# A decoder trunk in split fp32: the order of TensorE's products within groups of four weight blocks

## The reference

```python
def swiglu(h, w_in, w_out):
    gate, up = jnp.split(h @ w_in, 2, axis=-1)
    return (jax.nn.silu(gate) * up) @ w_out

for i in range(DEPTH):                     # DEPTH = 2, N_A = 1
    x = x + 0.5 * swiglu(rms_norm(x, ffn1_norm[i]), ffn1_w_in[i], ffn1_w_out[i])
    hm = rms_norm(x, mix_norm[i])
    if i < N_A:
        x = x + retention(hm, ret_w_in[i], ret_w_out[i])
    else:
        x = x + window_attention(hm, k_sh, v_sh, attn_w_q[j], q_norm[j], attn_sinks[j], attn_w_o[j])
    x = x + 0.5 * swiglu(rms_norm(x, ffn2_norm[i]), ffn2_w_in[i], ffn2_w_out[i])
    if i == N_A - 1:
        k_sh, v_sh = shared_kv(x, kv_norm, kv_w, k_norm)
```

## Time and profile before

| | us |
|---|---|
| median of 3 runs | 1044.52 (1043.75 to 1046.14) |
| profiled execution | 1044.49 |
| its span, first to last instruction | 1042.7 |
| PE busy | 1018.2 |
| PE weight loads busy | 884.8 |
| DVE busy | 797.1 |
| ACT busy | 499.4 |
| POOL busy | 110.0 |

### The profile page before, as it was taken

The page is one execution under the profiler, slowest core; times in us unless marked ns, Lnnn a source line. Parts: engine busy times, 40 slices in busy tenths (PEclk is TensorE's granted clock), DMA queues, the critical chain, the costliest instruction groups (busy, mean ns, idle before and its releaser), DMA issues.

```text
span 1042.7 us, 15888 instructions
## 1 busy us (share of the span) xinstructions
PE 1018.2 (98%) x5826; PEld 884.8 (85%) x5826; DVE 797.1 (76%) x953; ACT 499.4 (48%) x537; POOL 110.0 (11%) x102
## 2 busy tenths in 40 slices
PE   7999999999999999999999999999997699999998
PEld 6888888888888888888888888888886588888887
DVE  6977876788788688877766887788679768787743
ACT  5544544544444264544444455454447836454432
POOL 6000013201100151000023000001320040000000
PEclk9999999999999999999999999999998899999999
DMA  9655356652543454555456464544662134554461
GB/s 337 233 183 200 134 170 210 260 215 89 217 181 122 161 182 173 210 181 185 149 182 230 165 234 165 198 140 160 210 252 88 41 115 168 207 196 157 148 195 63
DMA packets 31281, 185.21 MB, mean 178 GB/s; under 512 B 3728, under 2 KB 5264, under 8 KB 14992
## 3 DMA queue, kind: packets, MB, share of 16 engines
q1 hardware_dynamic: 31248, 184.80, 49.9%
HBM read 183.73 MB, written 1.05 MB: 177 GB/s over the span
## 4 chain that ended last, share of the span: by engine, by line
PE 93%; DVE 3%; ACT 2%; DMA 1%; issue 0%; POOL 0%; SPq 0%; POOLq 0%; DVEq 0%; ACTq 0%
PE ps L1031 92%; PE ps L1294 1%; DMA stage<-w_in_dram 1%; ACT w_hi L301 1%; DVE h L625 1%; DVE w_lo L589 0%; ACT s_two L509 0%; DVE s_two L869 0%; ACT s_two L519 0%; ACT s_own L509 0%; DVE q_a L719 0%; DVE w_lo L949 0%; DVE q_b L716 0%; DVE s_own L869 0%; DVE q_a L713 0%
## 5 line engine op out<-in xcount | busy, mean ns | idle before, releaser
L1031 PE MATMUL ps<-h,w_hi 128*128 128x512 f32 x1664 | 585.3, 397 | 4.9 <-DVE h L625 3.0
L1031 PE MATMUL ps<-h,w_lo 128*128 128x256 f32 x1664 | 464.0, 279 | 0.0
L589 DVE TENSOR_TENSOR w_lo<-stage,w_hi 128x2048 fp32r<-128x2048 f32 (+1 forms) x191 | 399.1, 2098 | 29.5 <-ACT w_hi L301 29.2
L1031 PEld LDWEIGHTS ps<-h,w_hi 128*128 128x128 f32 x1664 | 313.3, 188 | 79.1 <-issue 3.3
L301 ACT ACTIVATE w_hi<-stage 128x2048 fp32r<-128x2048 f32 (+1 forms) x191 | 328.4, 1727 | 10.0 <-PE ps L1031 9.1
L1031 PEld LDWEIGHTS ps<-h,w_lo 128*128 128x128 f32 x1664 | 314.0, 189 | 0.3
L1031 PE MATMUL ps<-act_t,w_hi 128*128 128x512 f32 x704 | 245.4, 395 | 0.0
L1031 PE MATMUL ps<-act_t,w_lo 128*128 128x256 f32 x704 | 195.7, 278 | 0.0
L1031 PEld LDWEIGHTS ps<-act_t,w_hi 128*128 128x128 f32 x704 | 132.1, 188 | 31.3
L325 ACT ACTIVATE tmp<-ps 128x1024 f32<-128x1024 f32 x44 | 45.2, 1026 | 193.8 <-PE ps L1031 193.8
L1031 PEld LDWEIGHTS ps<-act_t,w_lo 128*128 128x128 f32 x704 | 132.3, 188 | 0.0
(11 more groups left out here) (150 smaller groups left out, 754.6 us busy)
## 6 DMA issues: line engine op xcount, KB each, us to landing
stage<-w_in_dram SPq DMA_DIRECT2D x86, 1024.0 KB, 4.8
stage<-w_out_dram SPq DMA_DIRECT2D x64, 704.0 KB, 4.1
stage<-w_ret_dram SPq DMA_DIRECT2D x24, 1024.0 KB, 4.8
stage<-w_ret_out_dram SPq DMA_DIRECT2D x8, 1024.0 KB, 4.8
stage<-w_q_dram SPq DMA_DIRECT2D x4, 1024.0 KB, 4.8
stage<-w_o_dram SPq DMA_DIRECT2D x4, 1024.0 KB, 4.9
stage<-w_in_dram SPq DMA_DIRECT2D x4, 256.0 KB, 6.1
x<-x_t_dram SPq DMA_DIRECT2D x4, 256.0 KB, 6.2
```

Of the source, the lines that this page charges most:

```text
L589: nc.vector.tensor_tensor(w_lo[:, s, 0:n], stage[:, s, 0:n], w_hi[:, s, 0:n].bitcast(F32), ALU.subtract).then_inc(lo_ready, 1)
L1031: return nc.tensor.matmul(out_, w, x_, start=start, stop=stop)
```

## The change

The helper `weight_block` is split into `hi_product` (the 512-column matmul) and `lo_product` (the 256-column one). All its callers take the blocks in groups of four: first the four 512-column matmuls, then the four 256-column ones. The w_out units with 11 blocks have groups of 4, 4 and 3. In `pair` a group is two tiles of h times two banks. Products, operands, banks and slots are the same, and each bank still gets its 512-column product first.

```diff
-            def weight_block(bank, slot, b, moving, first, last):
-
-                cols = slice(b * P, (b + 1) * P)
-                matmul(ps[:, bank, :], w_hi[:, slot, cols], moving, first, False)
-                return matmul(ps[:, bank, 0:T], w_lo[:, slot, cols], moving[:, 0:T], False, last)
+            def hi_product(bank, slot, b, moving, first):
+                return matmul(ps[:, bank, :], w_hi[:, slot, b * P:(b + 1) * P], moving, first, False)
+
+            def lo_product(bank, slot, b, moving, last):
+                return matmul(ps[:, bank, 0:T], w_lo[:, slot, b * P:(b + 1) * P], moving[:, 0:T], False, last)
...
                         for o in range(4):
-                            last = weight_block(4 * (g % 2) + o, (u + part) % SLOTS, 4 * k + o, h[:, kt, :],
-                                                kt == 0, kt == DT - 1)
+                            hi_product(4 * (g % 2) + o, (u + part) % SLOTS, 4 * k + o, h[:, kt, :], kt == 0)
+                        for o in range(4):
+                            last = lo_product(4 * (g % 2) + o, (u + part) % SLOTS, 4 * k + o, h[:, kt, :],
+                                              kt == DT - 1)
...
-                            for b in range(FT // 2):
-                                k = FT // 2 * part + b
-                                if d == 0 and k % 2 == 0:
-
-                                    if k in (0, 10, 18, 20):
+                            for b0 in range(0, FT // 2, 4):
+                                blocks = range(b0, min(b0 + 4, FT // 2))
+                                for b in blocks:
+                                    k = FT // 2 * part + b
+                                    if d == 0 and k in (0, 10, 18, 20):
+
                                         pe.wait_ge(a_ready, CREDIT + GROUPS * f + {0: 5, 10: 9, 18: 10, 20: 11}[k])
-                                last = weight_block(4 + d, u % SLOTS, b, act_t[:, k, :], k == 0, k == FT - 1)
+                                    hi_product(4 + d, u % SLOTS, b, act_t[:, k, :], k == 0)
+                                for b in blocks:
+                                    k = FT // 2 * part + b
+                                    last = lo_product(4 + d, u % SLOTS, b, act_t[:, k, :], k == FT - 1)
                             last.then_inc(used, 1)
...
-                for k in range(DT):
-                    if u == FIRST["ret", 0]:
-
-                        pe.wait_ge(h_lo, DT * RET + k + 1)
-                    for o in range(2):
-                        last = weight_block(banks + o, u % SLOTS, 2 * k + o, h[:, k, :], k == 0, k == DT - 1)
+                for k0 in range(0, DT, 2):
+                    blocks = [(k, o) for k in (k0, k0 + 1) for o in range(2)]
+                    for k, o in blocks:
+                        if u == FIRST["ret", 0] and o == 0:
+
+                            pe.wait_ge(h_lo, DT * RET + k + 1)
+                        hi_product(banks + o, u % SLOTS, 2 * k + o, h[:, k, :], k == 0)
+                    for k, o in blocks:
+                        last = lo_product(banks + o, u % SLOTS, 2 * k + o, h[:, k, :], k == DT - 1)
                 last.then_inc(used, 1)
```

More of the change, by code:

```diff
@@ L1206, in retention @@
                     pe.wait_ge(lo_ready, u0 + d + 1)
-                    for k in range(half):
-                        weight_block(d, (u0 + d) % SLOTS, k, y_t[:, k, :], k == 0, False)
+                    for k0 in range(0, half, 4):
+                        for k in range(k0, k0 + 4):
+                            hi_product(d, (u0 + d) % SLOTS, k, y_t[:, k, :], k == 0)
+                        for k in range(k0, k0 + 4):
+                            lo_product(d, (u0 + d) % SLOTS, k, y_t[:, k, :], False)
                     if d == 0:
@@ L1215, in retention @@
                         pe.wait_ge(lo_ready, u0 + d + 1)
-                    for k in range(half if d < 4 else 0, YT):
-                        last = weight_block(d, (u0 + d) % SLOTS, k, y_t[:, k, :], k == 0, k == YT - 1)
+                    for k0 in range(half if d < 4 else 0, YT, 4):
+                        for k in range(k0, k0 + 4):
+                            hi_product(d, (u0 + d) % SLOTS, k, y_t[:, k, :], k == 0)
+                        for k in range(k0, k0 + 4):
+                            last = lo_product(d, (u0 + d) % SLOTS, k, y_t[:, k, :], k == YT - 1)
                     last.then_inc(used, 1)
@@ L1324, in wo_unit @@
                         continue
-                    for k, kt in enumerate(kts):
-                        last = weight_block(d, u % SLOTS, len(kts) * n + k, o_t[:, kt, :], kt == 0, kt == DT - 1)
+                    for k0 in range(0, len(kts), 4):
+                        for k in range(k0, k0 + 4):
+                            hi_product(d, u % SLOTS, len(kts) * n + k, o_t[:, kts[k], :], kts[k] == 0)
+                        for k in range(k0, k0 + 4):
+                            last = lo_product(d, u % SLOTS, len(kts) * n + k, o_t[:, kts[k], :], kts[k] == DT - 1)
                     if j and d != tiles[-1]:
```

## The result

The changed kernel took 1050.14 us (median of six runs, 1047.11 to 1050.64), the kernel before 1044.24 in the same comparison. The ratio is 1.0047 with a 95% interval of 1.0034 to 1.0061: slower, by more than the 0.2% that a measurement of this kernel can tell. A second comparison in five rounds gave 1048.53 us and 1.0046 [1.0022, 1.0070]. The profiled execution took 1050.08 us, its span 1048.3.

A forecast was written before the change was run, and what follows sets the result against it. TensorE's distance between matmul starts was taken to bound the kernel. Terms 1 and 3 counted zero and term 2 saved 4.2 us, so 1044.49 became 1040.3 us, with a range of 1035.5 to 1050.

The forecast's parts named there:

- Term 1: Fast stretches: a group of four stays at 1387 ns, seams -7 to +13 ns a group, taken as zero; nothing gained.
- Term 2: Slow stretches in third FFN and retention heads: 632 blocks fall to the even step, 6.7 ns each, 4.2 us saved.
- Term 3: Waits for act_t (w_out units) and h (first retention unit) move up 0.12 and 0.24 us; slack covers them, no cost.
- the slow cadence spreads: New PSUM banks or seams slow 1928 weight blocks from 346.7 to 353 ns: 1057.3 us, mild form 1048.8; chance 0.22.
- The break-even: Weight blocks: the kernel averages 348.3 ns a block, so 1.6 ns over the even step decides between faster and slower.
- Seams give something back: Every 256-to-512 seam takes 0.113 us, unrepaid: 640 groups save another 6.7 ns each, 4.3 us, 1036.0 us; chance 0.12.
- Both cadences stay: Groups of four don't clear the entry's state; slow stretches stay slow, fast ones fast: 1044.5 us; chance 0.24.
- the mild case: Half the slow spread everywhere, 13.3 ns a group, 4.3 us more: 1048.8 us; half of the 0.22 chance.

## Why the prediction was wrong, point by point

**Term 1, the fast stretches, is the step that failed.** It held that equal-width steps would cost 226.7 and 120.0 inside a group and bounded the two seams from single steps, -7 to +13 ns a group, taking zero. Measured: +16.7 ns a group in w_in units, outside the bound, and some +9 in w_out units, inside its upper end but not zero. The bound looked at the one step on the seam. The disturbance behind a seam is five wide steps long, and a step ahead of it is no witness for the steps behind it. The rows had it: in the earlier trace rows the alternating stretch behind token_block begins with 0.23 and 0.11 and only then slows down. The sum "226.7 + 120.0 = 346.7, the fast cadence to the decimal" was a coincidence of totals: in the fast alternation no step is even (231, 112, 233, 117), and its long and short steps just cancel. Groups of four break that balance. Three FFNs lost 1.8 to 1.9 us each by it, 5.5 in all.

**Term 2, the slow stretches, was right in direction and too large.** The groups did end the slow cadence wherever it was, and in the FFNs one pace holds whatever the entry. But that pace is 350.8 and 349.1, not 346.7; the even step that it expected in each group is not reached by the wide products of a group of four. In the third FFN's w_in units the gain was 2.5 ns a block instead of 6.7, 0.8 us of 2.2, and in its w_out units 0.7 of 1.2. Retention, where 0.9 were expected, lost 0.3 with its output.

The profiled 1050.08 us is 9.8 over the forecast of 1040.3. By the traces 5.5 of that come from term 1; 1.8 in the third FFN and 1.1 in retention from what term 2 had promised; 1.2 from the start and 0.2 from attention, which the sum had not moved.

**Term 3 was right.** TensorE waits for no act_t anywhere in the changed kernel, and for h only in the start. It had left out that the wait of block 18 moves further than that of block 20, by three narrow products or 0.36 us; that operand was in time as well.

**The rivals.** The mild form of "the slow cadence spreads", 1048.8 us at a chance of half of 0.22, came nearest. Of its two mechanisms the second, a seam that throws the pipeline off, is close to what happens, although the pipeline goes into a disturbance of its own and not into the slow pattern; the first, a dearer step at each new bank, is refuted by the w_out units and by the two kernels without a change of width. The break-even it named, 1.6 ns over the even step, was passed with 4.2 in w_in and 2.5 in w_out units. "Seams give something back" was half true: the wide-to-narrow seam does return 8 ns, and the other takes 28. "Both cadences stay" was false in the trace, although its time would have been a closer guess than the forecast.

**The range** ended at 1050.0, a tenth of a microsecond under the median. It took in the mild case only at its single price of 1048.8. That price was half of an assumed worst case, so that it came near is luck, with the start of the program left as traced; the starts of the traces here differ by 2.7 us.

## What to carry to other kernels

When products of different widths take turns on TensorE, the price is in the sequence and not in the instruction. Read the distance between starts over several whole periods, and don't build a new sequence from single steps of an old one: the disturbance behind a change of width reaches five products on. Of the orders tried here none beat strict alternation in its fast cadence. Over that, a w_in unit cost 20 ns in runs of sixteen, 27 in twos, 40 in eights and 66 in threes and fours; in its slow cadence strict alternation cost 107. So look whether an alternating stretch is in its slow cadence. The order of small products ahead of it can cure that at no cost, and an added one did at 0.43 us; but an edit of one entry can turn other stretches slow, so the whole trace has to be read again.

## What the runs showed of the hardware

- An fp32r product with its own load, among products of the same width, steps at its columns over 2.4 GHz plus 13.3 ns: 226.7 for 512 and 120.0 for 256. The Trainium skill, page "TensorE: Matmul & The Clock Gate", section "Back-to-back issue gap", has N/2.4 + 2.5 ns for an isolated matmul's gap; the kernels without a change of width disagree with it for this kind of product, by 11 ns.
- Behind eight or more narrow products, a change from 256 to 512 columns costs 28 ns over five products, and a change back returns 8. Behind three narrow ones it cost 8 to 16. With 384 columns for 256, a round in groups of four costs 20 ns in w_in units and 31 in w_out units, over an even step that is itself an estimate.
- A strict alternation of 512 and 256 columns has two stable paces, 346.7 and 353.3 ns a pair, which hold for over 100 us. Reordering the small products ahead moved 328 blocks from the slow to the fast one; what in an entry decides is not shown. What holds them apart inside TensorE stays open.
